# One layer's small operations dealt out anew between VectorE and ScalarE, and ten expert weight parts on chip instead of nine

## The chip, the cores and the metric

The kernel runs on one core of a Trainium2 chip. TensorE (PE) multiplies matrices; VectorE (DVE) and ScalarE (ACT) work element by element; GpSimd (POOL) and SyncE (SP) mostly issue transfers here. The metric is the device time of one launch in microseconds (us), the median of several runs.

## The reference

Two blocks, one after the other, on 256 tokens of width 1024, all in float32. The first has two layers: an even one (gated convolution and chunked spatial gating) and an odd one, each followed by a feed-forward (`swiglu`, hidden width 2816) and a gated extra input. The second has one layer: a 31-tap convolution, then `hier_moe`, in which each token goes to 2 of 32 experts (hidden width 512), and a last norm. The odd layer's mixer is the place of the first part of the change:

```python
z = hn @ w_in                                  # q_lat, kv_lat, k_pe, mq, mk, mv, mo, mi, mf
q = rmsnorm(q_lat, g_qa) @ w_q_up              # 8 heads of 64 + 32
kv = rmsnorm(kv_lat, g_kva) @ w_kv_up          # 8 heads of 64 (k) + 64 (v)
q, k = per-head rmsnorm of both halves with gains, rotary turn of the 32
y_c = causal_softmax(q k^T) v
y_d = sigmoid(mo) * rmsnorm(mlstm(mq, mk, mv, mi + b, mf + b), g_mh)    # 4 heads, 128 wide
h = h + concat(y_c, y_d) @ w_out
```

An expert computes `(silu(x @ w_gate[e]) * (x @ w_up[e])) @ w_down[e]`; each of the three matrices of an expert is 2 MB.

## The kernel before

One program for each engine, all stages in the order of the reference. Dense matrix products go in three passes over weights split into a high and a low half: `split_hi` (ScalarE, L370) rounds a piece of 128x1024, `split_lo` (VectorE, L375) makes the remainder, and `tokens_by_columns` multiplies (L401 to L403). A buffer `ps` of eight banks takes all products. `own(...)` on VectorE waits for the instruction just issued.

The odd layer runs in these classes, called by each engine in this order:

- `OddIn`: `z`, in five items of up to 512 columns; `od_z` is filled by `scaled(i)`, token half 0 on ScalarE, half 1 on VectorE. Within it come the latents, the 24 products of q (`q_products`) and the squares and sums of q (`q_squares`).
- `OddUp`: 16 products of kv (`pe`, L1524), then the 8 transposes of the memory's q and k (L1530). ScalarE takes the exponential and the logarithm of the gates, then copies kv (L1424) and those transposes (L1427), and splits four pieces of `od_out`.
- `OddHeads`: VectorE (`dve`, L1574 to L1601) makes the gate sums, the inverse roots, the scaling and the rotary turn of q (L1574 to L1589), and after the copy of kv the squares, sums, root and two multiplications for k (L1597 to L1601). TensorE transposes q in four banks, then k in four (L1627); VectorE copies the even banks (L1606), ScalarE the odd ones (L1613). All four engines then meet in `stage_end`, a barrier.
- `OddAttend`: sums of the gates (L1659, L1660), `diag_b` (L1785), and a pipeline over 12 heads, 8 of attention and 4 of the memory. In each step TensorE does `scores` (L1679, L1680), `turn` (L1690) and `values` (L1709), VectorE `masked` (L1766 to L1778), ScalarE the exponentials (L1745) and `copy` (L1728). `memory_weights` (L1736), eight exponentials, stands after head 6. Another barrier ends it, after VectorE has divided the last four heads (L1835 to L1840).
- `OddOut`: a tanh (L1850), transposes of the mixed rows (L1899) in four banks, their split (L1854, L1860), the norm and gains of the memory's half (L1869 to L1880), and the product with `w_out`. The last two banks are made in `rest`, before the third piece of the first item.

The experts run in pairs (`ExpertsStage`): TensorE gathers the tokens (L2527), then gate and up of the two experts (L2538), then down (L2569). SyncE issues their weights in `weight_stream`, in one queue in a written order. There are three tiles for gate and up and three for down, which are 9 parts of 2 MB; `next_gate_up(e)` waits for expert e-3's gate and up to be used, and `next_down(e)` for the pair that holds expert e-3. The first parts wait for the last split of `conv_out` (and, but for the first expert, for the residual, `h_ready` 28).

## Time and profile before

| | |
|---|---|
| median of 3 runs | 1379.68 us (1378.28 to 1380.41) |
| the profiled execution | 1380.87 us, its span 1379.0 us |
| TensorE busy | 1262.5 us (92% of the span) |
| VectorE busy | 760.9 us (55%) |
| ScalarE busy | 482.7 us (35%) |
| chain that ended last | 76% TensorE, 10% VectorE, 7% transfers, 3% ScalarE |
| mean granted clock of TensorE | 0.961 |

Times within the profile are microseconds from the start of the span. The span is 1.9 us shorter than the execution's own time. In the page's strips the span is cut in 40 slices of 34.5 us; the odd layer's attention lies in slices 13 to 15, the experts in slices 27 to 40.

### The profile page before, as it was taken

What the parts mean: (1) busy time and instruction counts of PE and PEld (TensorE: products, weight loads), DVE (VectorE), ACT (ScalarE), POOL (GpSimd) and SP (SyncE); (2) the same over time, 40 slices, a digit from 0 to 9 for tenths busy, and PEclk for the clock granted to TensorE, in tenths of its full rate; (3) what the DMA queues carried; (4) which work ended last, traced back from release to release, by engine and by line L of the source; (5) the groups of instructions that cost most, each with busy time, mean ns of one, the idle gap of its engine ahead of it and who ended that gap; (6) DMA issues with size and microseconds to landing.
All of it is one profiled execution on the core that took longest, in us unless ns stands there. A gap on an engine that the chain in (4) does not pass through costs nothing.

```text
span 1379.0 us, 16368 instructions
## 1 busy us (share of the span) xinstructions
PE 1262.5 (92%) x6228; PEld 884.1 (64%) x6228; DVE 760.9 (55%) x1450; ACT 482.7 (35%) x806; POOL 27.0 (2%) x60
## 2 busy tenths in 40 slices
PE   6979999999896889999987998789999999999996
PEld 5967888876774667888875996554544454444442
DVE  5765877785657667777775998632122212222122
ACT  4424444444544335444444653411111111111111
POOL 0000000000000000000000300000000000000000
PEclk9989999999997689999999999889999999999999
DMA  8447766653421227777534320399999999999994
GB/s 272 149 153 287 268 244 244 243 183 137 169 95 51 92 87 285 267 254 254 194 110 150 122 77 1 150 424 418 414 432 427 429 432 431 431 429 429 432 430 186
DMA packets 113020, 354.42 MB, mean 257 GB/s; under 512 B 6762, under 2 KB 62755, under 8 KB 96578
## 3 DMA queue, kind: packets, MB, share of 16 engines
q1 hardware_dynamic: 106626, 328.48, 60.8%
q0 software_dynamic: 6336, 25.17, 4.6%
q8 instruction: 36, 0.59, 0.2%
q14 instruction: 22, 0.18, 0.0%
HBM read 352.58 MB, written 1.05 MB: 256 GB/s over the span
## 4 chain that ended last, share of the span: by engine, by line
PE 76%; DVE 10%; DMA 7%; ACT 3%; SPq 2%; issue 1%; DVEq 0%; ACTq 0%
PE ps L401 14%; PE ps L403 13%; PE ps L402 13%; PE ps L2538 13%; PE ps L2569 7%; PE ps L2527 4%; PE ps L2036 3%; DMA dense_weights<-in_moe_w_up 2%; DMA third_gate_up<-in_moe_w_up 2%; DMA second_expert<-in_moe_w_up 2%; DVE w_lo L375 1%; SPq L1053 1%; DMA dense_weights<-in_ev_w_in 1%; PE ps L2583 1%; PE ps L962 1%
## 5 line engine op out<-in xcount | busy, mean ns | idle before, releaser
L375 DVE TENSOR_TENSOR w_lo<-dense_weights,w_hi 128x1024 fp32r<-128x1024 f32 (+1 forms) x228 | 273.1, 1212 | 122.3 <-ACT w_hi L370 121.6
L370 ACT CAST w_hi<-dense_weights 128x1024 fp32r<-128x1024 f32 (+1 forms) x228 | 234.5, 1042 | 260.1 <-PE ps L403 236.3
L401 PE MATMUL ps<-w_hi,xT_lo 128*128 128x512 f32 (+1 forms) x624 | 251.1, 402 | 22.1 <-DVE xT_lo L2187 6.0
L403 PE MATMUL ps<-w_hi,xT_hi 128*128 128x512 f32 (+1 forms) x624 | 245.2, 393 | 0.0
L402 PE MATMUL ps<-w_lo,xT_hi 128*128 128x512 f32 (+1 forms) x624 | 245.1, 393 | 0.0
L401 PEld LDWEIGHTS ps<-w_hi,xT_lo 128*128 128x128 f32 x624 | 119.9, 192 | 51.1 <-issue 13.6
L403 PEld LDWEIGHTS ps<-w_hi,xT_hi 128*128 128x128 f32 x624 | 119.6, 192 | 25.4
L402 PEld LDWEIGHTS ps<-w_lo,xT_hi 128*128 128x128 f32 x624 | 120.2, 193 | 24.4 <-issue 0.7
L2676 DVE TENSOR_TENSOR hnT<-ps,g_bc 128x512 f32<-128x512 f32 x32 | 22.1, 692 | 163.5 <-PE ps L2569 163.5
L2685 DVE SCALAR_TENSOR_TENSOR cmask<-ge_th,ps 128x256 f32<-128x256 f32 x32 | 13.5, 422 | 163.0 <-ACT ge_th L2627 163.0
L2627 ACT ACTIVATE ge_th<-ps 128x256 f32<-128x256 f32 x32 | 12.3, 385 | 202.3 <-PE ps L2538 202.3
L2569 PE MATMUL ps<-dense_weights,g_mh 128*64 128x512 f32 x176 | 77.8, 595 | 3.8 <-issue 3.0
L2538 PE MATMUL ps<-dense_weights,ge_xT 128*64 128x512 f32 x352 | 77.8, 594 | 1.8 <-ACT ge_xT L2614 1.2
L2569 PE MATMUL ps<-second_expert,g_mh 128*64 128x512 f32 x176 | 77.8, 595 | 1.5 <-issue 1.5
L2538 PE MATMUL ps<-second_expert,ge_xT 128*64 128x512 f32 x352 | 77.7, 594 | 0.5 <-DMA second_expert<-in_moe_w_up 0.5
L401 PE MATMUL ps<-w_hi,ff_hidT_lo 128*128 128x512 f32 x176 | 68.7, 390 | 3.9 <-DVE ff_hidT_lo L933 3.9
L2569 PE MATMUL ps<-third_down,g_mh 128*64 128x512 f32 x160 | 70.8, 595 | 1.4 <-DMA dense_weights<-in_moe_w_down 1.4
L401 PE MATMUL ps<-xT_hi,w_lo 128*128 128x256 f32 x224 | 65.6, 293 | 6.3 <-DVE w_lo L375 3.4
L2538 PE MATMUL ps<-third_gate_up,ge_xT 128*64 128x512 f32 x320 | 70.7, 594 | 0.3 <-DMA third_gate_up<-in_moe_w_up 0.3
L403 PE MATMUL ps<-w_hi,ff_hidT_hi 128*128 128x512 f32 x176 | 68.5, 389 | 0.0
L402 PE MATMUL ps<-w_lo,ff_hidT_hi 128*128 128x512 f32 x176 | 68.5, 389 | 0.0
L402 PE MATMUL ps<-xT_lo,w_hi 128*128 128x256 f32 x224 | 64.7, 289 | 0.0
(404 smaller groups left out, 1778.0 us busy)
## 6 DMA issues: line engine op xcount, KB each, us to landing
ada_w<-in_ada_w POOLq DMA_DIRECT2D x12, 2048.0 KB, 12.2
dense_weights<-in_w_gate SPq DMA_DIRECT2D x22, 1024.0 KB, 7.1
dense_weights<-in_w_up SPq DMA_DIRECT2D x22, 1024.0 KB, 9.4
dense_weights<-in_w_down SPq DMA_DIRECT2D x22, 1024.0 KB, 5.0
dense_weights<-in_moe_w_gate SPq DMA_DIRECT2D x11, 2048.0 KB, 18.5
dense_weights<-in_moe_w_up SPq DMA_DIRECT2D x11, 2048.0 KB, 22.9
dense_weights<-in_moe_w_down SPq DMA_DIRECT2D x11, 2048.0 KB, 18.4
second_expert<-in_moe_w_gate SPq DMA_DIRECT2D x11, 2048.0 KB, 17.3
```

The costliest lines, as they stand in the source:

```text
L370: act.copy(split_view(w_hi, name, i, j), piece(name, i, j)).then_inc(hi_ready, 1)
L375: dve.tensor_tensor(split_view(w_lo, name, i, j), piece(name, i, j), split_view(w_hi, name, i, j).bitcast(F32), ALU.subtract).then_inc(pie ...
L401: pe.matmul(out, left[1], right[0], start=start, stop=False)
L402: pe.matmul(out, left[0], right[1], start=False, stop=False)
L403: return pe.matmul(out, left[0], right[0], start=False, stop=stop)
L962: last = pe.matmul(ps[:, 4 * i + 2 + t, :], pT[:, self.layer, k, t * P:(t + 1) * P], q[:, k, :], start=(k == 0), stop=(k == 1))
L1053: sp.dma_start(dst, src, allow_slow_non_contiguous=dst.dtype == I32).then_inc(small_landed, 16)
L2036: pe.matmul(ps[:, i, 0:S], diag[:, (i * TAPS + j) % DIAGS], u_pad[:, c, j:j + S], start=(j == 0), stop=(j == TAPS - 1)).then_inc(self.diag ...
L2527: last = pe.matmul(ps[:, 2 + k // 4, (k % 4) * P:(k % 4 + 1) * P], xn[:, t, k * P:(k + 1) * P], ge_sel[:, t], start=(t == 0), stop=(t == T ...
L2538: last = pe.matmul(out, ge_xT[:, k, e * PLACES:(e + 1) * PLACES], gate_up_rows(2 * p + e, k)[:, :, f * BLK:(f + 1) * BLK], start=(k == 0), ...
L2569: last = pe.matmul(ps[e * PLACES:(e + 1) * PLACES, n, :], ge_hidT[:, e, c, f * PLACES:(f + 1) * PLACES], down_rows(2 * p + e, 2 * f + c)[: ...
L2676: dve.tensor_tensor(ge_y[:, n], ps[:, n, :], g_bc[:, 1, n * 512:(n + 1) * 512], ALU.mult).then_inc(self.gated, 1)
```

## The change

There are two parts.

**The odd layer.** The two barriers go, and semaphores for single results stand in their place. VectorE makes the root and scaling of q (`q_factors`) before the last item's `scaled(4)`. TensorE does the memory's transposes ahead of the kv products, which are now released bank by bank. ScalarE takes over the squares of k, the copies of the rotary part, the copy of `v_aug` and the squares of the memory's norm; it makes an exponential of one element early, and copies all four q banks and two of k. The gain of k (`gk_col`) is multiplied in the copy after the transpose, for which three small operations are added at the start of `OddIn.dve`. The gate sums and `diag_b` are made before the transposes of k end. `memory_weights` is dealt out over heads 4 to 7. The first two banks of `OddOut` are transposed inside the last attention step. The tanh and the gains are prepared on the way, and the memory's norm ends with eight operations of 128x128 that release two halves.

**The experts.** A tenth part, expert 31's down, gets room of its own (`last_rows`, `last_piece`, half of `g_bc`), and some tiles are laid over others so that it fits. The down parts of experts 2 and 1 are issued during the convolution, expert 0's gate after the first item of `conv_out` is split, and expert 31's down right after expert 2's gate and up.

The diff, cut to its core (indentation shortened; renamed semaphores and the new places of tiles are left out):

```diff
@@ weight_stream
+    sp.wait_ge(conformer.diag_used, PE_TAPS)
+    down(2, None)
+    sp.wait_ge(conformer.normed, KC)
+    down(1, None)
+    wait_split("conv_out", 0, 3, None)
+    gate_or_up(0, None, 0)
     wait_split("conv_out", 1, 3, None)
-    gate_up(0, None)
...
     down(0, None)
     sp.wait_ge(h_ready, 28)
     gate_up(1, None)
-    down(1, None)
     gate_up(2, None)
-    down(2, None)
+    last = [d[:, LAST, half].rearrange("p c d -> p (c d)") for half in range(2)]
+    sp.dma_start(last_rows[:, 0:4].rearrange("p n d -> p (n d)"), last[0]).then_inc(last_landed, 16)
+    sp.dma_start(last_rows[:, 4], last[1][:, 0:512]).then_inc(last_landed, 16)
+    sp.dma_start(last_piece[:], last[1][:, 512:1024]).then_inc(last_landed, 16)
+    sp.dma_start(g_bc[:, 0], last[1][:, 1024:]).then_inc(last_landed, 16)
...
-        next_down(e, None)
-        if e + 1 < EXPERTS - 1:
+        if e + 1 < LAST:
+            next_down(e, None)
             next_down(e + 1, None)
 
-    e = EXPERTS - 1
+    e = LAST - 1
     sp.wait_ge(down_used, (e - TILES) // 2 + 1)
     for half in range(2):
         sp.dma_start(down_of(e).rearrange("p (h c) d -> p h c d", c=2)[:, half], d[:, e, half]
-                     ).then_inc(down_landed[(e + half) % TILES], 16)
+                     ).then_inc(b_landed[0] if half else down_landed[e % TILES], 16)
@@ OddIn.dve
+        wide = probT[:, 0, 0:QK]
+        own(dve.tensor_tensor(wide[:, 0:NOPE], ident[:, 0:NOPE], g_k[:, 0:NOPE], ALU.mult))
+        own(dve.tensor_copy(wide[:, NOPE:], ident[:, NOPE:QK]))
+        own(dve.tensor_reduce(gk_col, wide, AX.X, ALU.add))
...
+        odd_heads.q_factors(dve, own)
         scaled(4)
@@ OddUp.act
+        act.wait_ge(self.mqk_turned, 1)
+        act.copy(mqkT[:], ps[:, 2:4, :].rearrange("p b (c s) -> p (b c) s", c=2)).then_inc(self.mqk_freed, 1)
         act.wait_ge(self.gate_abs, 1)
         act.activation(lf[:, 0], lf[:, 0], ACT.Exp, scale=-1.0).then_inc(self.exps, 1)
...
-        split_upto(act, split_hi, "od_out", 0, 3, ahead=0)
+        for t in range(T):
+            key = act.copy(od_k[:, t, :, NOPE:], od_z[:, t, AT_KPE:AT_KPE + ROPE].unsqueeze(1).to_broadcast([P, HEADS, ROPE]))
+        key.then_inc(self.exps, 1)
+        act.activation(turns[:, 0, 0:1], lf[:, 0, 0, 0:1], ACT.Exp)
+        for g in range(4):
+            t, heads = g // 2, slice(g % 2 * (HEADS // 2), (g % 2 + 1) * (HEADS // 2))
+            made = ps[:, 4 + g, :].rearrange("p (h d) -> p h d", h=HEADS // 2)
+            act.wait_ge(up_used, g + 1)
+            act.activation(od_k[:, t, heads, 0:NOPE], made[:, :, 0:NOPE], ACT.Square, scale=float(NOPE) ** -0.5
+                           ).then_inc(self.kv_copied, 1)
+            act.copy(od_kv[:, t, heads, :], made).then_inc(self.kv_copied, 1)
@@ OddUp.pe
+        for c in range(4):
+            for t in range(T):
...
+        last.then_inc(self.mqk_turned, 1)
         wait_b(pe, "od_up", 0)
...
+                last.then_inc(up_used, 1)
@@ OddHeads
+    def q_factors(self, dve, own):
+        n, q3, sq = self.views()
+        for i, width in enumerate((NOPE, ROPE)):
+            own(dve.tensor_scalar(ms[:, i * n:(i + 1) * n], ms[:, i * n:(i + 1) * n], 1.0 / width, None, ALU.mult))
+        rsqrt_ms(dve, own, 2 * n)
+        dve.tensor_tensor(q3[:, :, 0:NOPE], q3[:, :, 0:NOPE], self.per_head(0, NOPE), ALU.mult)
+        own(dve.tensor_tensor(q3[:, :, NOPE:], q3[:, :, NOPE:], self.per_head(n, ROPE), ALU.mult))
+        own(dve.tensor_tensor(q3[:, :, NOPE:], q3[:, :, NOPE:], g_q[:, NOPE:].unsqueeze(1).to_broadcast([P, n, ROPE]), ALU.mult))
...
+        cut = slice(2 * n, 3 * n)
+        for g in range(4):
+            dve.wait_ge(self.up.kv_copied, 2 * g + 1)
+            at, half = 2 * n + g * (HEADS // 2), slice(g % 2 * (HEADS // 2), (g % 2 + 1) * (HEADS // 2))
+            own(dve.tensor_reduce(ms[:, at:at + HEADS // 2], od_k[:, g // 2, half, 0:NOPE], AX.X, ALU.add))
+        rsqrt(dve, own, ms[:, cut], rs[:, cut], rtmp[:, 0, cut], rtmp[:, 1, cut])
+        dve.wait_ge(self.up.kv_copied, 8)
+        dve.tensor_tensor(k3[:, :, 0:NOPE], kv3[:, :, 0:NOPE], self.per_head(2 * n, NOPE), ALU.mult).then_inc(self.k_ready, 1)
+        odd_attend.gate_columns(dve, own)
+        for b in (4, 6):
             dve.wait_ge(self.turned, b + 1)
+            dst = kT[0:QK, 2 * (b % 4):2 * (b % 4) + 2, :]
+            dve.tensor_scalar(dst, ps[0:QK, b, :].rearrange("p (h s) -> p h s", h=2), gk_col[0:QK], None, ALU.mult
+                              ).then_inc(self.dve_copied, 1)
+    def act(self, act):
+        for b in (0, 1, 2, 3, 5, 7):
+            if b == 5:
+                split_upto(act, split_hi, "od_out", 0, 3, ahead=0)
...
+            act.activation(dst, src, ACT.Copy, scale=1.0 if b < 4 else gk_col[0:QK]).then_inc(self.act_copied, 1)
@@ OddHeads.pe
+                pe.wait_ge(self.q_ready, T)
+            if b == 4:
+                odd_attend.pe_sums(pe)
+                pe.wait_ge(self.k_ready, 1)
+                pe.wait_ge(self.up.exps, 3)
+            if b == 7:
+                pe.wait_ge(odd_attend.diag, 1)
@@ OddAttend
+    def pe_sums(self, pe):
+        pe.wait_ge(odd_heads.q_ready, T + 1)
+        pe.wait_ge(odd_heads.up.kv_copied, 8)
         for t in range(T):
-            o = ps[:, 5, t * MH:(t + 1) * MH]
+            o = ps[:, 7, t * MH:(t + 1) * MH]
             if t:
                 pe.matmul(o, ones[:], lf[:, 2, 0], start=True, stop=False)
             last = pe.matmul(o, upper[:], lf[:, 2, t], start=(t == 0), stop=True)
         last.then_inc(self.cum, 1)
...
+    def gate_columns(self, dve, own):
+        dve.wait_ge(self.cum, 1)
+        own(dve.tensor_copy(acum[:], ps[:, 7, 0:T * MH].rearrange("p (t h) -> p t h", t=T)))
+        own(dve.tensor_tensor(bcol[:], gts[:, :, 0:MH], acum[:], ALU.subtract))
+        for t in range(T):
...
+                              bcol[:, t].unsqueeze(2).to_broadcast([P, MH, P]), ALU.mult).then_inc(self.diag, 1)
...
+        pe.wait_ge(odd_heads.act_copied, 6)
+        pe.wait_ge(odd_heads.dve_copied, 2)
@@ OddAttend.pe
+            if step == self.N:
+                for b in range(2):
+                    odd_out.turn(pe, b)
@@ OddAttend.act
+        def memory_weights(m):
+            if m == 0:
+                act.wait_ge(self.mx, 1)
+                act.activation(emt[:], emt[:], ACT.Exp, scale=-1.0)
+            for t in range(T):
+                b = b_masked[:, m, 0:P] if t == 0 else b_masked[:, m, P:3 * P]
+                last = act.activation(b, b, ACT.Exp, bias=nmax[:, HEADS + m, t:t + 1])
+            last.then_inc(self.w_mem, 1)
+        act.wait_ge(odd_heads.turned, 4)
+        act.copy(v_aug[:, :, :, 0:MV], od_z[:, :, AT_MV:AT_MO].rearrange("p t (h d) -> p t h d", h=MH)).then_inc(self.v_aug_ready, 1)
...
+            if hd >= HEADS - MH:
+                memory_weights(hd - (HEADS - MH))
+        odd_out.gate(act)
@@ OddAttend.dve
+                dve.wait_ge(self.w_mem, m + 1)
...
-        def values():
...
-                   7: lambda: split(2), 9: lambda: split(3)}
+        between = {1: lambda: rows(0), 2: lambda: rows(1), 3: maxima, 5: lambda: split(0), 7: lambda: split(1),
+                   8: lambda: split(2), 10: lambda: split(3)}
+        dve.memset(v_aug[:, :, :, MV:], 1.0).then_inc(self.v_aug_ready, 1)
...
+        odd_out.gains(dve, own)
         for m in range(MH):
+            if m == 3:
+                for b in range(2):
+                    odd_out.low(dve, b)
...
-            own(dve.tensor_copy(den[:, 0], num[:, :, MV]))
-            own(dve.tensor_scalar(den[:, 1], den[:, 0], -1.0, None, ALU.mult))
-            own(dve.tensor_tensor(den[:, 0], den[:, 0], den[:, 1], ALU.max))
-            own(dve.tensor_tensor(den[:, 0], den[:, 0], emt[:, :, m], ALU.max))
+            own(dve.tensor_tensor(den[:, 0], num[:, :, MV], emt[:, :, m], ALU.max))
+            own(dve.scalar_tensor_tensor(out=den[:, 0], in0=num[:, :, MV], scalar=-1.0, in1=den[:, 0], op0=ALU.mult, op1=ALU.max))
             own(dve.reciprocal(den[:, 0], den[:, 0]))
...
-        stage_end(dve)
@@ OddOut
+    def gate(self, act):
+        act.activation(od_z[:, :, self.gains_at], od_z[:, :, AT_MO:AT_MI], ACT.Tanh, scale=0.5).then_inc(self.tanh, 1)
...
+        dve.wait_ge(self.tanh, 1)
+        g = od_z[:, :, self.gains_at]
+        own(dve.scalar_tensor_tensor(out=g, in0=g, scalar=1.0, in1=g_mh[:].unsqueeze(1).to_broadcast([P, T, MH * MV]),
+                                     op0=ALU.add, op1=ALU.mult))
...
+        def high(b):
             act.wait_ge(self.turned, b + 1)
...
+        for b in range(2):
+            high(b)
+        junk = od_kv[:].rearrange("p t h d -> p t (h d)")[:, :, 0:MH * MV].rearrange("p t (h d) -> p t h d", h=MH)
+        for m in range(MH):
+            act.wait_ge(odd_attend.y_freed, T + m + 1)
+            for t in range(T):
+                act.activation(junk[:, t, m], y_d[:, t, m, :], ACT.Square, scale=float(MV) ** -0.5,
+                               accum_out=ms[:, t * MH + m:t * MH + m + 1]).then_inc(self.tanh, 1)
+        for b in range(2, 4):
+            high(b)
...
-        def low(b):
...
-        for b in range(2):
-            low(b)
-        split_upto(dve, split_lo, "od_out", 0, 1, ahead=0)
         n = T * MH
-        sq = od_kv[:].rearrange("p t h d -> p t (h d)")[:, :, 0:MH * MV].rearrange("p t (h d) -> p t h d", h=MH)
-        own(dve.tensor_tensor(sq, y_d, y_d, ALU.mult))
-        own(dve.tensor_reduce(ms[:, 0:n].rearrange("p (t h) -> p t h", t=T), sq, AX.X, ALU.add))
-        own(dve.tensor_scalar(ms[:, 0:n], ms[:, 0:n], 1.0 / MV, None, ALU.mult))
+        dve.wait_ge(self.tanh, 1 + n)
         rsqrt_ms(dve, own, n)
         own(dve.tensor_scalar(rs[:, 0:n], rs[:, 0:n], 0.5, None, ALU.mult))
-        for t in range(T):
-            own(dve.tensor_tensor(y_d[:, t], y_d[:, t],
-                                  rs[:, t * MH:(t + 1) * MH].unsqueeze(2).to_broadcast([P, MH, MV]), ALU.mult))
-        flat = mix[:, :, HEADS * VD:]
-        own(dve.tensor_tensor(flat, flat, g_mh[:].unsqueeze(1).to_broadcast([P, T, MH * MV]), ALU.mult))
-        dve.wait_ge(self.tanh, 1)
-        dve.scalar_tensor_tensor(out=flat, in0=od_z[:, :, AT_MV:AT_MO], scalar=1.0, in1=flat, op0=ALU.add,
-                                 op1=ALU.mult).then_inc(self.y, 1)
+        g = od_z[:, :, self.gains_at].rearrange("p t (h d) -> p t h d", h=MH)
+        for m in range(MH):
+            for t in range(T):
+                last = dve.scalar_tensor_tensor(out=y_d[:, t, m, :], in0=y_d[:, t, m, :], scalar=rs[:, t * MH + m:t * MH + m + 1],
+                                                in1=g[:, t, m, :], op0=ALU.mult, op1=ALU.mult)
+            if m % 2 == 1:
...
         def rest():
-
-            pe.wait_ge(self.y, 1)
-            turn((2, 3))
+            for b in (2, 3):
+                pe.wait_ge(self.y, b - 1)
+                self.turn(pe, b)
             pe.wait_ge(self.lo, 4)
 
-        turn((0, 1))
```

## Rows read from the trace of the kernel before

**Rows 1.** The page's strips, 40 slices of the span: granted clock and bytes moved.

```profile
PEclk9989999999997689999999999889999999999999
...
GB/s 272 149 153 287 268 244 244 243 183 137 169 95 51 92 87 285 267 254 254 194 110 150 122 77 1 150 424 418 414 432 427 429 432 431 431 429 429 432 430 186
```

**Rows 2.** Windows in the attention; us, then busy by engine, clock, DMA share, GB/s.

```profile
447.00:452.00 5.00, 4.50 (x30) 3.28 (x29) 4.37 (x10) 2.88 (x11) 0.00 (x0) 1.00 0.00 2
465.00:470.00 5.00, 5.00 (x20) 4.23 (x21) 1.33 (x2) 0.96 (x2) 0.00 (x0) 0.50 0.01 2
```

**Rows 3.** Timeline of VectorE, odd layer: start, us, line, operation, idle before and releaser.

```profile
357.77 0.22 DVE L1340 TENSOR_TENSOR g_k<-g_k,g_q 128x64 f32<-128x64 f32 x1
...
414.76 0.39 DVE L1346 TENSOR_SCALAR od_z<-ps,rstd 128x168 f32<-128x168 f32 x1 [3.74 <-PE ps L403]
...
418.40 1.22 DVE L1574 TENSOR_TENSOR od_q<-od_q,rs 128x1024 f32<-128x1024 f32 x1
...
420.99 0.29 DVE L1584 TENSOR_TENSOR xn<-od_q,cs 128x128 f32<-128x128 f32 x1
...
424.73 1.22 DVE L1597 TENSOR_TENSOR xn<-od_kv 128x1024 f32<-128x1024 f32 x1
...
430.86 1.23 DVE L1601 TENSOR_TENSOR od_k<-od_k,g_k 128x1024 f32<-128x1024 f32 x1
...
439.03 0.55 DVE L1766 SCALAR_TENSOR_TENSOR sm<-ps,cmask 128x384 f32<-128x384 f32 x1
...
485.92 1.22 DVE L1869 TENSOR_TENSOR od_kv<-xn 128x1024 f32<-128x1024 f32 x1
...
493.58 1.23 DVE L1880 SCALAR_TENSOR_TENSOR xn<-od_z,xn 128x1024 f32<-128x1024 f32 x1
```

**Rows 4.** Timeline of ScalarE, odd layer.

```profile
421.66 1.87 ACT L1424 COPY od_kv<-ps 128x2048 f32<-128x2048 f32 x1 [3.46 <-PE ps L1524]
...
440.31 1.28 ACT L1745 ACT_TABLE_LOAD   x1 [3.90 <-DVE nmax L1771]
441.60 0.40 ACT L1745 ACTIVATE prob<-sm,nmax 128x128 f32<-128x128 f32 x1
...
461.09 2.87 ACT L1736 ACTIVATE od_k<-od_k,nmax 128x128 f32<-128x128 f32 x8
```

**Rows 5.** Timeline of TensorE, odd layer.

```profile
421.46 1.04 PE L1530 MATMUL ps<-ident,od_z 128*128 128x128 f32 x8
...
432.14 3.65 PE L1627 MATMUL ps<-ident,od_k 128*96 128x128 f32 x16 [4.52 <-DVE od_k L1601]
...
437.18 0.47 PE L1679 MATMUL ps<-mixT,hnT 96*128 96x128 f32 x2
...
464.99 0.90 PE L1690 MATMUL ps<-ident,prob 128*128 128x128 f32 x3 [1.56 <-ACT prob L1745]
...
483.04 1.62 PE L1899 MATMUL ps<-ident,xn 128*128 128x128 f32 x8 [2.30 <-DVEq L318]
486.06 0.79 PE L401 MATMUL ps<-w_hi,xT_lo 128*128 128x512 f32 x1 [1.40 <-DVE xT_lo L1860]
...
497.58 0.79 PE L401 MATMUL ps<-w_hi,xT_lo 128*128 128x512 f32 x1 [1.56 <-DVE xT_lo L1860]
```

**Rows 6.** The chain of waits in order of time, experts: start, us, what.

```profile
977.98 6.87 PE ps L2538 x32
...
1005.34 6.87 PE ps L2538 x32
...
1341.66 6.87 PE ps L2538 x32
```

**Rows 7.** Timeline of SyncE's queue, experts.

```profile
882.59 0.34 SPq L570 DMA_DIRECT2D dense_weights<-in_moe_w_gate  x1
...
978.03 0.38 SPq L573 DMA_DIRECT2D third_down<-in_moe_w_down  x1
```

**Rows 8.** One window of the experts, columns as in rows 2.

```profile
978.00:980.00 2.00, 2.00 (x12) 0.61 (x10) 1.84 (x3) 0.72 (x1) 0.00 (x0) 1.00 0.85 225
```

221 lines of the change are left out of this document (84 added, 137 removed).

## The prediction

> **What bounds the kernel now.** I read the page's strips first, then the granted clock by stretches, the timelines of the three engines through the odd layer, and last the chain, the queue and the windows of the experts. The strips show two places where TensorE isn't at its best: slices 13 to 15, where the granted clock falls to 6 tenths and little is moved, and the experts, where the clock is full and some 430 GB/s flow without a break [rows 1]. The odd layer's attention is the first. TensorE alternates there between its two levels: 2.4 GHz in 447 to 452, 1.2 GHz in 465 to 470, where it is busy for all 5.00 us [rows 2]. Around that, VectorE and ScalarE hold it up. The reader is to see in VectorE's timeline that it stands still for 3.74 us before the copy at 414.76 and then works almost without a break until k is ready at 432.1 (430.86 + 1.23) [rows 3]; in ScalarE's, that a table load stands before the first softmax [rows 4]; and in TensorE's, the waits of 4.52, 1.56, 2.30, 1.40 and 1.56 us [rows 5].
>
> The sum is made in the profiled execution's clock (1380.9 us, span 1379.0 and 1.9 around it), which is 1.2 above the median of 1379.7. I take differences alone and set them off the median.
>
> **The odd layer, step by step.** Times are on the clock of before.
>
> *Start, +0.7.* Three operations of 64 to 96 columns are put ahead of the first weight split, on which TensorE waits. The nearest takes 0.22 [rows 3]; with `own` between them, three make 0.7 (0.6 to 0.8). Nothing hides them.
>
> *q.* From 414.76 to 418.40 VectorE does the copy (about 0.5 with its wait), three gate operations (0.6) and the root (2.6); the scaling runs from 418.40 to 420.99, 2.6 more [rows 3]. The 5.2 of root and scaling now begin at 411.0, in the idle 3.74, so they push the copy by 1.5: gates at 417.3, and with the 12 small rotary operations (2.95 of the 3.74 between 420.99 and 424.73) q is ready at 420.2, not 423.9. TensorE has the 8 transposes (1.04) first, then the 16 products (414.6 to 421.46 before, 7.0 [rows 5]), so until 422.7; q is hidden by them. The q transposes follow at once, until 425.6.
>
> *k.* ScalarE decides. It copies the transposes from 415.7 (1.0, about half of the 1.87 for 2048 columns), then takes a table load (1.28) and a small function (0.2) twice, to 419.9, the key copies (0.6) to 420.5, and the early exponential with a third load (1.5) to 422.0. Then come four squares of 256 (0.36, the mean of the eight in 2.87) and four copies of 512 (0.47, a quarter of 1.87): 3.3, to 425.3 [rows 4]. If no two of them overlap, 4.0. VectorE adds the last sum (0.4 after the last square, 425.3), the root (2.1) and one multiplication (1.22): k is ready at 428.7 instead of 432.1, 3.4 earlier. Before, squares, sum, root and two multiplications took from 424.73 to 432.1 [rows 3].
>
> *To the first scores, -4.1 in all.* The transposes of k take 3.65 as before, ScalarE's last copy 0.6: 433.0. The sums of the gates (0.7, after that copy before; scores began at 437.18 [rows 5]) now lie ahead of k. `diag_b` and both VectorE copies end at 432.2, and the four splits that ScalarE has between q and k (3.9) end at 431.2, before the last bank is turned. So scores begin at 433.1.
>
> *To the first exponential, -2.1.* Before, `masked` began at 439.03, 1.85 after the scores did, because `diag_b` was in front; the scores alone need about 1.0, so 0.85 go. The table load of 1.28 goes as well: the early exponential has paid it beside the kv products. ScalarE's `v_aug` copy (1.0) fits before 435.3.
>
> A rule speaks against this. The Trainium skill (ScalarE: Activation LUTs, What ACT_TABLE_LOAD costs) puts a switch at about 2.66 us, with a drain of 1.38 beside the load. Here the activation behind the load at 440.31 starts at 441.60, 0.01 after the load's end [rows 4], so the trace has no drain there. An estimate by the page: three switches ahead of the squares make k 4.1 later, the load taken off the softmax gives 1.4 more, and the sum is 7.5 instead of 10.2.
>
> *Heads, -0.85.* The wait of 1.56 behind the eight exponentials (2.87) goes. Dealt out, each pair costs 0.72 behind a copy. Where TensorE runs at 1.2 GHz it is full, and the 0.72 are hidden; at head 5 it isn't, so +0.7 once. Without that cover the four would cost 2.9 in all, which is the bound.
>
> *To the product, -1.9.* Eight transposes (1.62) move ahead of the last two `values`, which then end at 483.0; before, they and the waits of 2.30 and 1.40 lay between that and 486.06 [rows 5]. VectorE has the gains (1.23) in front of the divisions and two remainders (1.3) in the middle, but each division has lost two of six operations. The remainders end at 484.1 and the product starts at 484.2. The last division ends at 485.1.
>
> *Second wait, -1.5 and clock -0.4.* Before, the norm ran from 485.92 to 494.8 on VectorE, and TensorE resumed at 497.58, 11.5 after its start [rows 3, 5]. Now the squares of the last head (0.85, ScalarE), a root (2.3) and eight operations of 128x128 (0.29 each [rows 3], 0.22 when they follow each other: 1.8) end at 490.1, before the 7.5 of products do at 491.7. The four transposes of each bank (1.05 together), the rounding (0.6) and two remainders (1.3, half beside it) bring TensorE back at 494.15, 3.4 earlier in all. The gap is shorter, and the low level after it may stay out: the first matmuls after 497.58 follow at 0.43 us, where 0.23 is normal, 1.4 in all. I take 0.4 between 0 and 1.4.
>
> The sum: +0.7 - 4.1 - 2.1 - 0.85 - 1.9 - 1.5 - 0.4 = -10.2.
>
> **The experts, 0.** A pair takes 27.36 us of TensorE (977.98 to 1005.34). From 977.98 to 1341.66 are 13 pairs, 355.7, and 8.0 more [rows 6]. Six parts of 2.1 MB at 430 GB/s take 29.3, so transfers set the pace once the lead is used up, and those 8.0 are what the tenth part could win. But the lead isn't kept. Nine parts of 4.9 us from 882.59 are in at 926.5, when no tile is free; the next ten are in by 978, and the queue then stands before expert 5's down, which needs the pair before it to be done: it is issued at 978.03 [rows 7], and in 978 to 980 only 225 GB/s flow [rows 8]. So the queue has run empty, with 9 parts on chip. After the change three parts are in before 882.6 and the rest by 917, but the tiles free up at the same moments, and from 927 on the same parts follow in the same order. Only expert 31's down is gone from the end, 4.9 us of transfer for which TensorE doesn't wait in this trace. The early parts cost nothing: SyncE has nothing behind its new waits, and the bus is empty between 843 and 882. Bounds: -8.0, and +0.5 if a landing slips.
>
> The forecast is 1379.7 - 10.2 = 1369.5 us.
>
> **Rivals.** *The experts' waits go too:* 1369.5 - 8.0 = 1361.5. For it speaks that transfers end the waits late in the stage; against it, the empty queue at 978. Chance 0.10.
> *TensorE stays at 1.2 GHz in attention:* the ten microseconds around 447 to 452 at full clock hold four heads; at 3.3 us a head, as in the full stretch [rows 2], instead of 2.4, +3.6 to +4: 1373.5. More is put on ScalarE and TensorE's steps are spaced anew. Chance 0.18.
> *It stays at 2.4 GHz:* the 24 us from 457 to 481 are seven steps of 3.4; heads would fall to ScalarE's 2.75, the memory's to 2.2: -7, 1362.5. Chance 0.10.
> *ScalarE becomes the bound:* its squares and copies don't overlap (+0.7) and each copy, exponential and pair of weights stands in the chain of every head (+2.9), the remainders wait for its rounding (+1.5): 1374.6. Chance 0.10.
> *Table loads drain the engine* (the rule above, as a mechanism: ScalarE would stand for as long again after each of three loads): about 1372.2. Chance 0.02; the row at 440.31 is against it.
> *Slower:* TensorE stays at 1.2 GHz from the first turn of q to the end of `od_out`. Its 96 products of 512 columns take 0.43 instead of 0.23, of which some 16 do so already: +16, and +4 in the heads: 1379.7 - 10.2 + 20 = 1389.5. It decides from some 50 slow products on. Against it: after 486.06 the level rose within 10 products. Chance 0.05.
>
> **How the numbers follow.** The forecast has 0.45 and a range of its own of 1367.5 to 1371.5. From 1361.5 to 1376 the range takes in all but the slow rival and the ends of the others. A difference of 0.2%, 2.8 us, is about what a measurement of this kernel can tell from none. Faster by more: 0.90, all but the last rival and a small part of the fourth; within: 0.05; slower: 0.05.
>
> **What would show it.** Three more VectorE operations before 362 and od_in 0.7 later; k ready some 14 us after od_in's last product instead of 17.5; no table load before the first softmax, which starts 6.2 sooner after od_in; no wait of 1.5 at head 7; the product's second wait below 2.5 us. In the experts, a queue empty for some 10 us before the first release, and the same 8.0 of waits over 13 pairs. Wrong would be the forecast if the granted clock in slices 13 to 15 differs from before, or if those 8.0 shrink.

## The result

| | median | ratio to the kernel before, with its 95% interval |
|---|---|---|
| before (4 runs beside it) | 1379.36 us | |
| changed | 1369.34 us (1368.00 to 1370.70, 4 runs) | 0.9914 [0.9894, 0.9934] |

By the medians that is 10.0 us less, where 10.2 were forecast (1369.5); the ratio gives 11.9 (9.1 to 14.6). The sum was right. Its parts were not: the profiled execution (1369.42 us, span 1367.6) shows a larger gain in the odd layer and two small losses behind it. Differences below are between the two profiled spans. Of all executions named below one, of `end_barrier`, was slow (1690.6 us, mean granted clock 0.732) and is left out.

### The profile page after: what moved, and what is told of

Its sections match the earlier page's. It is cut to its first block, busy times and chain, and to the rows that moved or that the text cites. A ratio compares the mean times of both kernels' runs of the same rounds, so it can differ in the third digit from the quotient of the medians.

```text
span 1367.6 us, 16386 instructions
## 1 busy us (share of the span) xinstructions
PE 1260.3 (92%) x6228; PEld 882.6 (65%) x6228; DVE 752.9 (55%) x1442; ACT 489.2 (36%) x835; POOL 26.9 (2%) x60
## 4 chain that ended last, share of the span: by engine, by line
PE 79%; DVE 9%; DMA 7%; ACT 4%; issue 1%; SPq 1%; DVEq 0%; ACTq 0%
PE ps L404 14%; PE ps L406 14%; PE ps L405 14%; PE ps L2591 13%; PE ps L2622 7%; PE ps L2580 4%; PE ps L2089 3%; DMA dense_weights<-in_moe_w_up 2%; DMA third_gate_up<-in_moe_w_up 2%; DMA second_expert<-in_moe_w_up 2%; DVE w_lo L378 1%; PE ps L2636 1%; PE ps L987 1%; PE ps L2637 1%; PE ps L1765 1%
## 5 line engine op out<-in xcount | busy, mean ns | idle before, releaser
L2738 DVE SCALAR_TENSOR_TENSOR cmask<-g_v,ps 128x256 f32<-128x256 f32 x32 | 13.5, 421 | 162.3 <-ACT g_v L2680 162.3
L2680 ACT ACTIVATE g_v<-ps 128x256 f32<-128x256 f32 x32 | 12.3, 383 | 202.3 <-PE ps L2591 202.3
L2622 PE MATMUL ps<-second_expert,g_mh 128*64 128x512 f32 x160 | 70.7, 595 | 2.2 <-issue 2.2
```

What stands on the lines that cost most here:

```text
L2622: last = pe.matmul(ps[e * PLACES:(e + 1) * PLACES, n, :], ge_hidT[:, e, c, f * PLACES:(f + 1) * PLACES], down_rows(2 * p + e, 2 * f + c, n ...
```

## The profile after

The page's strips of the changed kernel, granted clock and bytes moved, answer to [rows 1].

```profile
PEclk9989999999998699999998999899999999999999
...
GB/s 274 151 143 300 256 253 252 246 185 100 166 128 62 93 178 255 252 252 254 192 124 124 124 63 62 317 316 418 412 429 428 430 431 430 430 432 427 432 429 119
```

Slices 13 to 15 read 8, 6, 9, where the kernel before has 7, 6, 8: the clock there is not the same, which the prediction had named as a sign against itself. The slices are 34.2 us long where they were 34.5, so part of this can be the cut. "Level" below is the granted clock of TensorE, 1.2 or 2.4 GHz. Windows of 3 us in the attention show where it falls and where it comes back (as [rows 2]: us, busy time of PE, PEld, DVE, ACT, POOL, clock, DMA share, GB/s).

```profile
443.00:446.00 3.00, 2.34 (x20) 1.94 (x19) 2.93 (x7) 1.60 (x6) 0.00 (x0) 1.00 0.00 0
446.00:449.00 3.00, 1.43 (x11) 1.02 (x10) 2.86 (x10) 1.32 (x5) 0.00 (x0) 1.00 0.00 0
449.00:452.00 3.00, 2.09 (x16) 1.69 (x15) 2.06 (x4) 2.15 (x8) 0.00 (x0) 0.76 0.00 0
452.00:455.00 3.00, 3.00 (x14) 2.67 (x14) 0.00 (x0) 2.05 (x7) 0.00 (x0) 0.50 0.00 0
...
473.00:476.00 3.00, 2.47 (x16) 2.27 (x14) 1.17 (x6) 2.33 (x11) 0.00 (x0) 0.75 1.07 414
476.00:479.00 3.00, 1.90 (x8) 1.59 (x9) 2.10 (x8) 1.27 (x8) 0.00 (x0) 1.00 0.27 109
```

TensorE is at 2.4 GHz while it waits between the heads (busy for 1.43 of 3 us), falls to 1.2 GHz in the window from 449, is busy all the time from 452 on, and the level comes back in the window from 473, just ahead of the product. VectorE's timeline, for [rows 3]:

```profile
357.78 0.22 DVE L1365 TENSOR_TENSOR g_k<-g_k,g_q 128x64 f32<-128x64 f32 x1
...
358.51 0.25 DVE L1370 TENSOR_REDUCE ms<-probT 128x1 f32<-128x96 f32 x1
...
427.80 1.22 DVE L1637 TENSOR_TENSOR od_k<-od_kv,rs 128x1024 f32<-128x1024 f32 x1
...
434.25 0.56 DVE L1821 SCALAR_TENSOR_TENSOR sm<-ps,cmask 128x384 f32<-128x384 f32 x1 [2.28 <-PE ps L1736]
...
480.96 2.19 DVE L1939 SCALAR_TENSOR_TENSOR xn<-xn,rs,od_z 128x128 f32<-128x128 f32 x8
```

ScalarE's, for [rows 4]. The table load now stands ahead of the squares, and the first softmax has none:

```profile
421.10 1.28 ACT L1462 ACT_TABLE_LOAD   x1
422.39 0.20 ACT L1462 ACTIVATE turns<-lf 128x1 f32<-128x1 f32 x1
422.50 0.37 ACT L1467 ACTIVATE od_k<-ps 128x256 f32<-128x256 f32 x1
...
435.49 0.40 ACT L1805 ACTIVATE prob<-sm,nmax 128x128 f32<-128x128 f32 x1 [2.04 <-DVE nmax L1826]
```

TensorE's, for [rows 5], from the first split of `od_in` to the first wait of the second feed-forward layer:

```profile
364.00 0.50 PE L404 MATMUL ps<-w_hi,xT_lo 128*128 128x512 f32 x1 [1.82 <-DVE w_lo L378]
...
429.08 2.71 PE L1670 MATMUL ps<-ident,od_k 128*96 128x128 f32 x16 [2.51 <-DVE od_k L1637]
...
432.56 0.80 PE L1735 MATMUL ps<-mixT,hnT 96*128 96x128 f32 x2 [0.77 <-ACT mixT L1652]
...
477.10 0.50 PE L404 MATMUL ps<-w_hi,xT_lo 128*128 128x512 f32 x1 [1.63 <-DVE xT_lo L1928]
477.44 0.39 PE L405 MATMUL ps<-w_lo,xT_hi 128*128 128x512 f32 x1
...
485.28 0.50 PE L404 MATMUL ps<-w_hi,xT_lo 128*128 128x512 f32 x1 [1.42 <-DVE xT_lo L1928]
...
518.50 0.47 PE L404 MATMUL ps<-w_hi,xT_lo 128*128 128x512 f32 x1 [2.26 <-DVE ff_hid L949]
...
519.61 0.63 PE L404 MATMUL ps<-w_hi,xT_lo 128*128 128x512 f32 x1
```

From 477.44 products follow each other at 0.23 us; before, eight of them took 0.43. At 518.50 the same wait as before (2.26 us) is followed by seven products at 0.43, which the kernel before doesn't have: 1.5 us are lost there. So the feed-forward layer starts 13.65 us earlier than before, the experts only 12.1. The chain, the queue and a window in the experts, for [rows 6 to 8]:

```profile
965.85 6.87 PE ps L2591 x32
...
1330.23 6.87 PE ps L2591 x32
```

```profile
884.19 0.46 SPq L616 DMA_DIRECT2D g_bc<-in_moe_w_down  x1
...
915.12 0.34 SPq L581 DMA_DIRECT2D dense_weights<-in_moe_w_gate  x1
...
965.89 0.38 SPq L588 DMA_DIRECT2D third_down<-in_moe_w_down  x1
```

```profile
904.00:914.00 10.00, 8.75 (x51) 5.00 (x52) 1.06 (x6) 1.01 (x1) 0.00 (x0) 0.97 0.42 166
...
965.80:967.80 2.00, 2.00 (x12) 0.59 (x10) 1.77 (x3) 0.72 (x1) 0.00 (x0) 1.00 0.74 234
```

Nothing is issued between 884.19 and 915.12, and from 904 to 914 only 166 GB/s flow: the queue is empty well before the first tile comes free, and empty again at 965.8. Over the 13 pairs TensorE waits 1330.23 - 965.85 - 13 x 27.36 = 8.7 us, where it was 8.0.

## The experiments

Each kernel is the changed one with one edit, unless it says otherwise. Ratios are to the kernel before, run beside it. "turn(11)" is the start of the last head's transposes; "first turn to turn(11)" is the length of the attention. The odd layer's code is the same in the changed kernel and in runs 1 and 2, and the executions still differ: the six of run 1 go from 1362.06 to 1371.32 us. So a step that is read from one trace alone is uncertain by its level.

**1. The odd layer alone** (`odd_only`): the experts' stream as before.

```
-            down(2, None)
...
-            down(1, None)
...
-            gate_or_up(0, None, 0)
             wait_split("conv_out", 1, 3, None)
-            gate_or_up(0, None, 1)
+            gate_up(0, None)
             down(0, None)
             sp.wait_ge(h_ready, 28)
             gate_up(1, None)
+            down(1, None)
             gate_up(2, None)
-            last = [d[:, LAST, half].rearrange("p c d -> p (c d)") for half in range(2)]
...
+            down(2, None)
```

> The changed kernel with the experts' weight stream of before: no early loads, no tenth part. My theory (the experts' part is worth nothing): the same as the changed kernel, 1369 to 1370 us, and the same waits of about 8.5 us over the 13 pairs. Rival (the tenth part pays at the end of the stream and is hidden by something that grew): slower than the changed kernel by 2 to 5 us, about 1373, with a wait ahead of the last down. Second rival (the early loads disturb the stages before the experts): faster than the changed kernel by about 1 us.

Measured: 1369.6 us, 0.9910 [0.9888, 0.9932]. In its trace the 13 pairs take 363.87 us, so 8.2 of waits. The interval is nearly that of the changed kernel. The experts' part of the change is worth nothing that can be measured; the first theory holds.

**2. The tenth part for expert 9** (`part_for_9`): the same buffer, loaded at the same time, with other weights. The first rounds of the loops are written out so that expert 9 can be left out of the stream.

```
-            if e == LAST:
+            if e == KEEP and it is None:
                 return last_pieces[2 * c + n]
...
-            last = [d[:, LAST, half].rearrange("p c d -> p (c d)") for half in range(2)]
+            last = [d[:, KEEP, half].rearrange("p c d -> p (c d)") for half in range(2)]
...
+                for made in (e, e + 1):
+                    if made != KEEP:
+                        next_down(made, None)
+            with sp.Fori(2, loops) as it:
```

> The tenth part holds expert 9's down weights instead of expert 31's, so that it is left out of the stream in the middle, after the queue has run empty for the last time (965.8 in the changed kernel's trace) and before the first wait for weights (1151). My theory (only a part that the queue would have to carry ahead of a waiting pair is worth its 4.9 us): the first wait comes some 2.5 pairs later and the waits over the 13 pairs fall from 8.7 to about 4, so 1364.5 us. Rival (the waits come from the way tiles are released, not from the sum of transfers): no change, 1369.3. Rival (the pair's code outside the loop has to be fetched): slower by some us.

Measured: 1365.52 us, 0.9886 [0.9867, 0.9904]. Timeline of its queue, the two ends of the 13 pairs and two issues between, each at the end of a pair:

```profile
966.40 0.38 SPq L591 DMA_DIRECT2D third_down<-in_moe_w_down  x1
...
1212.64 0.38 SPq L591 DMA_DIRECT2D third_down<-in_moe_w_down  x1
...
1241.38 0.38 SPq L591 DMA_DIRECT2D second_expert<-in_moe_w_down  x1
...
1325.68 0.80 SPq L646 DMA_DIRECT2D second_expert<-in_moe_w_down  x2
```

The pairs run in 27.36 us up to 1212.64; the first that takes longer (28.7) ends at 1241.38, three pairs later than the first wait of the changed kernel. 1325.68 - 966.40 - 355.68 = 3.6 us of waits. One part of 2.1 MB is worth 5 us of waits here where it was worth none for expert 31, as expected. It repeats: in the traces of the eleven kernels without this edit the 13 pairs have 7.9 to 9.2 us of waits, in the two of run 8, which have it, 4.2 and 5.6. The medians of runs 1 and 2, taken side by side, are 4.1 apart. Writing the first rounds out without moving the part wasn't run by itself.

**3. The small operations behind the splits** (`angles_later`).

```
-                own(dve.tensor_tensor(g_k[:, 0:NOPE], g_k[:, 0:NOPE], g_q[:, 0:NOPE], ALU.mult))
-
-                wide = probT[:, 0, 0:QK]
...
-                self.up.turns_of(dve, own, self.freq)
...
                 split_upto(dve, split_lo, "od_in", 0, 3)
+                self.up.turns_of(dve, own, self.freq)
                 scaled(0)
+                own(dve.tensor_tensor(g_k[:, 0:NOPE], g_k[:, 0:NOPE], g_q[:, 0:NOPE], ALU.mult))
+                wide = probT[:, 0, 0:QK]
```

> VectorE's 5 us of small operations ahead of the first od_in split (three of them new with the change) are moved behind the four splits and the first scaled copy. By my term of +0.7 for three of them, all of them stand on the path up to the wait of 1.82 us that TensorE has before od_in's second piece: that wait goes, and the granted clock, which falls to the low level for about 8 products behind it, may stay up: -1.8 to -3.4 us, 1366 to 1367.5. Rival (another split or ScalarE's rounding is late at once): -0.8 or less.

Measured: 1363.26 us, 0.9879 [0.9864, 0.9894], 4.8 us below the changed kernel by the ratios. Its windows over the second piece of `od_in`:

```profile
361.54:367.54 6.00, 6.00 (x28) 4.95 (x28) 5.28 (x25) 3.92 (x5) 0.00 (x0) 1.00 0.66 255
```

The changed kernel, in the window of the same length behind its wait:

```profile
364.00:370.00 6.00, 6.00 (x19) 4.79 (x20) 4.10 (x4) 1.49 (x2) 0.00 (x0) 0.72 0.83 286
```

No wait, and the clock 1.00 instead of 0.72: 28 matmuls where there were 19. From the transposes ahead of `od_in` to its last product it takes 59.97 us instead of 64.18, so 4.2 less, of which 1.8 are the wait. The gain is larger than the 3.4 that I gave at most; the first theory holds in kind. But with the operations in front this stretch takes 62.4 to 64.6 us in the traces of runs 1, 2 and 4 to 7, so the gain is 2.5 to 4.7. It hangs on the level: in run 2 the wait is 1.61 us and the clock behind it stays up.

```profile
364.11:370.11 6.00, 6.00 (x26) 4.99 (x27) 4.01 (x4) 2.92 (x4) 0.00 (x0) 1.00 0.85 283
```

It also bears on my term for the start: what stands ahead of that split is on the path, and can cost more than the wait that it makes.

**4. Dummy products in the attention** (`fill`): they write a bank that nobody reads.

```
+                    if 4 <= step < 12:
+                        if step == 4:
+                            pe.wait_ge(self.rows_freed, T)
+                        for _ in range(1):
+                            pe.matmul(ps[:, 5, 0:3 * P], ident[:], cmask[:], start=True, stop=True)
```

> One dummy product of 128x384 (identity times the mask, into a PSUM bank that nobody reads) is put behind each turn from the fourth step of the attention on, eight in all; nothing else is changed. If TensorE's level in the attention hangs on how much TensorE works before, as the low level from 451 on behind the waits of 443 to 449 suggests, the clock stays up through the heads and they fall to ScalarE's pace: the first turn to turn(11) takes 29 to 31 us instead of 34.6, so -4 to -5 us in all. Rival (the level falls anyway): each filler costs up to 1.3 us at the low level where TensorE is full, so +5 to +8 us.

Measured: 1362.59 us, 0.9872 [0.9855, 0.9890], 5.8 us below the changed kernel by the ratios. Windows, where the changed kernel falls and where it is low:

```profile
449.00:452.00 3.00, 2.73 (x17) 2.07 (x18) 1.89 (x3) 2.15 (x8) 0.00 (x0) 1.00 0.00 0
452.00:455.00 3.00, 2.83 (x19) 2.17 (x18) 1.35 (x5) 2.05 (x7) 0.00 (x0) 1.00 0.00 0
...
461.00:464.00 3.00, 3.00 (x20) 2.23 (x19) 2.39 (x5) 0.48 (x1) 0.00 (x0) 1.00 0.01 3
```

The level stays at 2.4 GHz up to the end of the layer, so the first theory holds. First turn to turn(11) takes 32.26 us, above the 29 to 31 that I expected, because the level still is low at the first heads; the same attention took 34.60 in the changed kernel's trace and 36.98 in those of runs 1 and 2. The filled heads are shorter by 2.3 to 4.7 us, although TensorE does more work; the eight traces of the changed kernel and its variants without fillers have 34.4 to 37.0. From turn(11) to the product it is 4.63 instead of 5.97.

**5. The end of the attention in the old order** (`end_no_order`), **and with a barrier** (`end_barrier`).

```
-                    if step == self.N:
-                        for b in range(2):
-                            odd_out.turn(pe, b)
...
-                    if m == 3:
-                        for b in range(2):
-                            odd_out.low(dve, b)
...
+                for b in range(2):
+                    self.turn(pe, b)
                 pe.wait_ge(self.lo, 2)
```

The second has, besides, at the end of the attention's code of TensorE, ScalarE and VectorE:

```
+            eng.drain().then_inc(odd_attend.cum, 1)
+            eng.wait_ge(odd_attend.cum, 4)
```

> The changed kernel with the end of the attention in the old order: the eight transposes of banks 0 and 1 behind the last values, the two remainders behind the last division; no barrier. It undoes my term 'to the product'. My theory: the product starts 1.9 to 2.3 us later after turn(11) (7.9 to 8.3 instead of 5.97), its second wait is as short as before, and if the granted clock falls in the gap as in the kernel before, some ten products cost 0.2 each more: +2 to +4 us, 1371.5 to 1373. Rival (the gain came from the cheaper divisions alone): the product starts less than 0.7 later.

> The same, with TensorE, ScalarE and VectorE drained and made to wait for each other at the end of the attention, as before the change. If the barrier costs by itself: the transposes wait for the last division (478 in the changed kernel's trace), so the product starts about 1.4 to 2 us later still than without it, 1373 to 1375. Rival (the barrier is free because TensorE waits for the last division anyway in this order): the same as the run without it, within 0.5 us from turn(11) to the product.

Measured: 1370.46 us, 0.9932 [0.9911, 0.9952] without the barrier, 1371.89 us, 0.9949 [0.9931, 0.9967] with it. TensorE's timeline without it:

```profile
479.34 0.51 PE L404 MATMUL ps<-w_hi,xT_lo 128*128 128x512 f32 x1 [1.61 <-DVE xT_lo L1922]
...
487.50 0.50 PE L404 MATMUL ps<-w_hi,xT_lo 128*128 128x512 f32 x1 [1.56 <-DVE xT_lo L1922]
```

and with it:

```profile
475.83 1.10 PE L1962 MATMUL ps<-ident,xn 128*128 128x128 f32 x8 [1.38 <-DVEq L326]
478.62 0.80 PE L409 MATMUL ps<-w_hi,xT_lo 128*128 128x512 f32 x1 [1.69 <-DVE xT_lo L1930]
479.21 0.63 PE L410 MATMUL ps<-w_lo,xT_hi 128*128 128x512 f32 x1
...
489.40 0.50 PE L409 MATMUL ps<-w_hi,xT_lo 128*128 128x512 f32 x1 [1.56 <-DVE xT_lo L1930]
```

turn(11) starts at 473.29 and 470.93. From there to the product are 6.05 us without the barrier (5.80 to 5.97 in the changed kernel and runs 1 to 3, with the new order; 5.46 and 5.17 in runs 6 and 7, where the level is back sooner) and 7.69 with it; from the product to its resumption 8.16 and 10.78, since with the barrier the level falls and a dozen products take 0.43 us. So the order of the transposes is worth 0.1 to 0.25 us on the path, and the time difference of the first run to the changed kernel, whose intervals overlap, isn't seen there. My theory for it fell: I had expected about 2. In these two traces the barrier costs 1.6 us of waiting and 2.6 of clock. In exchange the fall behind the feed-forward layer's first wait stays out, which gives some 1.5 of the 4.3 back. The ratios differ by 0.0017, 2.3 us, but their intervals overlap, so the price of the barrier is read from traces and isn't shown by the times.

**6. The memory's exponentials in one lump** (`mem_lump`), **and that with the dummy products** (`fill_and_lump`).

```
-                    if hd >= HEADS - MH:
-                        memory_weights(hd - (HEADS - MH))
+                    if hd == HEADS - 2:
+                        for m in range(MH):
+                            memory_weights(m)
```

> The changed kernel with the eight exponentials of the memory's weights in one lump behind head 6 again. It undoes my term 'heads, -0.85': the wait of 1.56 comes back and the 0.7 go, so the first turn to turn(11) takes 35.4 us instead of 34.6 and the time is 1370.2. Rival (dealing them out costs as much as it saves, since it lengthens ScalarE's chain in head 5, where the level falls): no difference, or up to 1 us faster.

Measured: 1367.49 us, 0.9916 [0.9896, 0.9935], no difference from 0.9914. The wait is back:

```profile
457.65 0.90 PE L1746 MATMUL ps<-ident,prob 128*128 128x128 f32 x3 [1.56 <-ACT prob L1805]
```

From turn(4), at 447.24, to turn(11), at 470.50, are 23.26 us; in the changed kernel 448.72 to 471.13, 22.41. That is the -0.85 of my term; that it fits to the hundredth is luck. The attention as a whole takes 35.27, which I had forecast (35.4), but against 34.60, and the same code has 36.98 elsewhere. To the product it is 5.46 instead of 5.97, since the level is back 1 us sooner behind turn(11), and from `od_in` to the feed-forward layer both take 89.8 (92.2 and 92.0 in runs 1 and 2).

> The changed kernel with the eight dummy products and with the memory's exponentials in one lump behind head 6. By itself the lump cost nothing that could be measured (0.9916 against 0.9914). My theory: it was hidden because TensorE is at its low level, and full, at that time; at full clock the wait behind the lump (2.20 us in the run of the kernel before with fillers) stands on the path and lets the level fall behind it, as there. First turn to turn(11) 35 to 38 us instead of 32.3 with fillers alone, and 3 to 5 us slower than that, a ratio of 0.989 to 0.991. Rival (the level stays up): only the wait's 1.5 to 2.2 us, a ratio of 0.988 to 0.989.

Measured: 1365.30 us, 0.9896 [0.9872, 0.9921], where `fill` has 0.9872. TensorE waits 2.21 us behind the lump, and the clock of the window with that wait is 1.00:

```profile
456.00:459.00 3.00, 0.96 (x6) 0.52 (x4) 2.36 (x3) 3.00 (x11) 0.00 (x0) 1.00 0.00 0
```

First turn to turn(11) takes 33.80, 1.5 more than with fillers alone; the level is low over the first heads, as in `fill`, and up from there to the end of the attention. So where the clock is full, dealing the exponentials out is worth 1.5 us in the traces; the intervals of the two runs overlap. The level's fall, which I had expected, didn't come in the heads; one comes later, behind the feed-forward layer's first wait.

**7. The table load behind the squares** (`k_sooner`).

```
-
-                act.activation(turns[:, 0, 0:1], lf[:, 0, 0, 0:1], ACT.Exp)
                 for g in range(4):
...
+                act.activation(turns[:, 0, 0:1], lf[:, 0, 0, 0:1], ACT.Exp)
...
-                        split_upto(act, split_hi, "od_out", 0, 3, ahead=0)
+                        split_upto(act, split_hi, "od_out", 0, 1, ahead=0)
...
+                    if hd in (5, 6):
+                        split_upto(act, split_hi, "od_out", 0, hd - 3, ahead=0)
```

> The early exponential with its table load of 1.28 us is moved from ahead of the four squares to behind them, and two of ScalarE's four splits between q and k are moved into the heads. My step 'ScalarE decides when k is ready': the squares start 1.3 to 1.5 sooner, k is ready at 427.5 instead of 429.0 in the changed kernel's clock, and the scores and first softmax come 1.3 to 1.6 sooner, 1367.8 us. Rival (the products of k and v end at 423.1 and set the last square, or the heads lose by the two splits what the start gains): -0.5 to +0.5 us. Rival (VectorE sets k): k ready unchanged.

Measured: 1364.45 us, 0.9899 [0.9877, 0.9920], 2.1 us below the changed kernel by the ratios, with overlapping intervals. ScalarE's timeline, where the load stands now:

```profile
420.03 0.37 ACT L1465 ACTIVATE od_k<-ps 128x256 f32<-128x256 f32 x1
...
423.22 1.28 ACT L1468 ACT_TABLE_LOAD   x1
424.51 0.20 ACT L1468 ACTIVATE turns<-lf 128x1 f32<-128x1 f32 x1
```

The transposes of k start 12.37 us after `od_in`'s last product instead of 13.85, which is the same to 0.01 in every trace with the load in front, and the first softmax 17.66 instead of 20.26 (20.1 to 20.5 in the others). ScalarE decides when k is ready, as the prediction had it. Here too the fall behind the feed-forward layer's first wait stays out, which is worth some 1.5 us and isn't shown to be the edit's doing.

**8. All four together** (`all_four`: runs 2, 3, 4 and 7), **and five fillers more** (`more_fill`).

```
                         odd_attend.pe_sums(pe)
+                        for _ in range(3):
+                            pe.matmul(ps[:, 4, 0:3 * P], ident[:], cmask[:], start=True, stop=True)
...
+                    if step == 1:
+                        for _ in range(2):
+                            pe.matmul(ps[:, 5, 0:3 * P], ident[:], cmask[:], start=True, stop=True)
```

> The changed kernel with the tenth part for expert 9, the angles behind the splits, the early exponential behind the squares, and the eight dummy products in the attention. If the four gains lie at different places and add, their ratios to the kernel before (0.9886, 0.9879, 0.9899 and 0.9872, against 0.9914 for the changed kernel) give 0.979 to 0.980, some 1351 us; if the clock's part of them is shared (it is the same low stretch that moves in three of them), 1353 to 1356.

> The same with five dummy products more: three behind the gates' sums, while TensorE waits for k, and two ahead of the first turn. If the low stretch at the first scores (some 10 us in the traces of the changed kernel and of the run with eight fillers) also hangs on TensorE's idle time before it, the scores and the first heads run at full clock: -1.5 to -3 us against the run before it. Rival (the level follows something else, or the fillers delay the first turn): -0.3 to +1.3 us.

Measured: 1353.57 us, 0.9811 [0.9798, 0.9825], and 1351.69 us, 0.9790 [0.9777, 0.9803]. The first lies in the second of its two expectations, that the clock's part of the gains is partly the same; its interval takes in the upper end of the first, so that isn't decided. In its trace the scores (at 430.25) and the first heads already run at full clock, and the level is low only around the transposes of k:

```profile
427.00:430.00 3.00, 2.47 (x14) 2.12 (x12) 2.10 (x5) 2.19 (x4) 0.00 (x0) 0.66 0.00 0
```

With five fillers more it is up there too, and the scores start 15.47 us behind `od_in`'s last product instead of 16.49:

```profile
427.00:430.00 3.00, 2.36 (x11) 1.88 (x12) 1.79 (x6) 1.68 (x4) 0.00 (x0) 1.00 0.02 5
430.00:433.00 3.00, 2.63 (x12) 1.31 (x11) 1.56 (x5) 2.18 (x9) 0.00 (x0) 1.00 0.00 0
```

The fall behind the feed-forward layer's first wait is gone as well. But `k_sooner` has 15.46 and no such fall without any filler, so what the five are worth isn't shown; the intervals of the two runs just overlap.

`more_fill` beats both kernels: 2.1% below the kernel before, 1.2% below the changed one.

**9. The dummy products in the kernel before** (`fill_before`).

```
+                    if 4 <= step < 12:
+                        if step == 4:
+                            pe.wait_ge(self.rows_freed, T)
+                        pe.matmul(ps[:, 5, 0:3 * P], ident[:], cmask[:], start=True, stop=True)
```

> The kernel before with the same eight dummy products in the attention. If the low stretch is not of the change's making but of the waits between the heads: first turn to turn(11) in 32 to 33 us instead of 35.19, and the low levels behind 484 stay or go with the barrier's wait; -2.5 to -5 us, a ratio of 0.9965 to 0.998. Rival (the stretch in the kernel before has another cause): slower by up to 8 us.

Measured: 1377.62 us, 0.9979 [0.9969, 0.9988], 0.2% or some 2.9 us faster. Its profiled execution is the slowest of ten (1381.65), slower than the median of the kernel before, and shows where the gain can be lost. The level is up longer than before, until TensorE stands behind the lump of exponentials (2.20 us), and falls there:

```profile
461.00:464.00 3.00, 0.86 (x4) 0.86 (x5) 0.56 (x1) 2.08 (x9) 0.00 (x0) 0.81 0.00 0
464.00:467.00 3.00, 3.00 (x11) 2.28 (x10) 0.00 (x0) 0.48 (x1) 0.00 (x0) 0.50 0.01 3
```

First turn to turn(11) takes 38.30 in that execution, not the 32 to 33 that I expected. The gain over ten runs is real, but its place isn't shown by this trace. Low levels behind the barrier are there as before. That the lump of exponentials is why fillers do less here than in the changed kernel is argued from this trace; `fill_and_lump` has the same lump and a wait of 2.21 us without the fall.

## Why the prediction was right

By its steps, in the two profiled spans:

| step | predicted | measured |
|---|---|---|
| start | +0.7 | +0.8 |
| to the first scores | -4.1 | -5.4 |
| to the first exponential | -2.1 | -1.5 |
| heads | -0.85 | -0.6 |
| to the product | -1.9 | -2.3 |
| second wait and clock | -1.9 | -3.3 and -1.35 |
| between odd layer and experts | 0 | +1.5 |
| experts | 0 | +0.7 |
| sum | -10.2 | -11.4 (medians: -10.0) |

The parts miss by up to 2.8 us, in both directions, and cancel. That the sum came within 0.2 us of the medians is luck, and by its own sign, the clock in slices 13 to 15, it ought to have missed; that the change gains, and by a size like this, follows from the steps that are found right below.

*Start.* Right: `g_k` is multiplied at the same moment (357.78 and 357.77), and TensorE resumes at 364.00 instead of 363.22. Run 3 shows that more than these three operations is on that path.

*To the first exponential.* Right in mechanism. The transposes of k start 13.85 us after `od_in`'s last product, where 17.7 were before and some 14 forecast. The 5.4 and 1.5 are the two terms as this trace divides them, 6.9 together for 6.2. In run 1, with the same code, the scores stand 18.16 behind that product instead of 17.33 and the exponential 20.36 instead of 20.26, so only their sum is worth comparing. One size was carried over wrongly: the transposes of k took 3.65 before, and take 2.71 here and 3.52 in run 1, by how much of them falls on the low level. Run 7 confirms who decides.

*Table loads.* The rival with a drain is out. The load at 421.10 ends at 422.38 and the next activation starts at 422.39; in run 7 it is 424.50 and 424.51. The Trainium skill (ScalarE: Activation LUTs, What ACT_TABLE_LOAD costs) has 1.38 us more for a switch; no load of the odd layer shows it in any of these traces: where ScalarE waits for no other engine, 0.01 to 0.03 us lie ahead of each and as much behind. The measurement decides.

*Heads.* Right as a local term (run 6), and of little use to the sum: the same attention code took 34.60, 36.98 and 36.98 us in three traces, by where the level fell. That the profiled execution has 34.60 is luck; with 36.98 the heads would have been a loss of 1.8. The term is a third of a spread that I had taken as nothing.

*To the product.* The size is near, the reason was wrong. I gave the 1.9 to the transposes moved ahead; run 5 gives them 0.1 to 0.25 and the barrier 1.6. With the barrier and the old order it takes 7.69 of the 8.23 of before, so all that the divisions lost and the gains added comes to 0.5.

*Second wait and clock.* This is the term that was mis-sized, 1.9 for 4.7. The step that failed is the clock: the sum let the first products take "the 7.5" that they had before, and took 0.4 for the level behind the second wait. From the product's start to its resumption were 11.52 us before and are 8.18 now. The last matmul ahead of the gap, before and after, divides them:

```profile
493.38 0.39 PE L403 MATMUL ps<-w_hi,xT_hi 128*128 128x512 f32 x1
...
482.45 0.40 PE L406 MATMUL ps<-w_hi,xT_hi 128*128 128x512 f32 x1
```

From the product's start it is 5.35 us up to there instead of 7.32, and the gap behind them 2.83 instead of 4.20. So the shorter norm gave 1.4, for which I had 1.5, and the clock 2.0 in the first products and 1.35 behind the second wait, 3.3 where I had 0.4. In run 5's traces the level there hangs on the barrier: with it the first part takes 7.95, and the gap the same 2.83. The order matters. In `fill_before`, with the old norm, the first part takes 6.72 and the resumption still comes after 11.52: a faster product was worth nothing there, since VectorE's norm ends last.

*Behind the odd layer.* That some of it would be lost again wasn't in the sum. The fall behind the wait at 518.50 cost 1.5 us, where the kernel before had its low stretch earlier, at 497.58. There is no such fall in `fill`, `end_barrier`, `k_sooner` and `more_fill`, and there is one in the other seven variants of the changed kernel. What brings it isn't shown.

*The experts.* Right, and shown by run 1. The reason is shown by run 2: the tenth part is worth 5 us when the queue would have to carry it between its last empty moment and the last wait, and nothing for the last expert. The 0.7 more of waits lie within what such runs differ by (7.9 to 9.2 us in all traces without run 2's edit).

The rivals on TensorE's level gave one level to the whole stretch each. The measured attention has both, as before. The 2.4 GHz rival, 1362.5, is near what the fillers bring (1362.59), but there only part of the gain lies in the heads. The rival with ScalarE as the bound (1374.6) and the slower one didn't come.

## What to carry to other kernels

A barrier, or any wait of TensorE between short steps, can cost more than itself, since the level may fall behind it (here 1.6 us of waiting and 2.6 of clock, in one trace). A few products that nobody reads can keep the level up: eight were worth 5.8 us in the changed kernel, and 2.9 in the kernel before. A buffer that keeps weights on chip pays only for weights that the queue would otherwise carry between the last moment it is empty and the last wait for it, so find both in the queue's timeline before choosing what to keep.
